# Chains between products: scaling of the stream on VectorE, a root of the mean per token on a 128x2 tile, sums turned by halves, and two weight units split ahead

## The reference, cut to what matters

```python
for l in range(2):                                   # first block
    xm = rms_norm(x, norm_mix_w[l]) * (1 + sc1) + sh1
    proj = xm @ w_in[l]                              # q, k, v, pool, gates: 4096 columns
    ...                                              # attention, pooling, gates
    x = x + g1 * (merged @ w_out[l])
    xf = rms_norm(x, norm_ffn_w[l]) * (1 + sc2) + sh2
    x = x + g2 * peer_ffn(xf, ...)                   # query, top-k, all 16384 experts as dense products
x = rms_norm(x, final_norm_w)

def post_norm_update(x, y, gate, res_w, g, b):       # second block: after each of six sub-layers
    return layer_norm(ALPHA * x + res_w * gate * y, g, b)
# per layer: half-step FFN, mixer (neighbourhood attention in layer 0, short convolution in layer 1), half-step FFN
# FFN: (silu(a) * u) @ w_out with a, u = split((x * (1 + scale) + shift) @ w_in); in layer 0 the context passes the first FFN too
```

## Time and profile before

| | us |
|---|---|
| median of 3 runs | 3928.18 |
| lowest and highest run | 3926.26, 3933.19 |
| profiled execution, its own time | 3927.0 |
| its span, first to last instruction | 3925.1 |
| TensorE busy / VectorE / ScalarE / GpSimd | 3737.5 / 2533.5 / 2049.0 / 231.4 |

### The profile page before, as it was taken

How to read it: one execution, slowest core, us unless ns; L and a number is a source line. 1 busy time by engine, 2 the same in 40 slices (tenths; PEclk the granted TensorE clock), 3 DMA queues, 4 the chain that set the end, 5 groups by cost and what they waited for, 6 DMA issues and landing times.

```text
span 3925.1 us, 75611 instructions
## 1 busy us (share of the span) xinstructions
PE 3737.5 (95%) x26204; PEld 3326.8 (85%) x26204; DVE 2533.5 (65%) x4978; ACT 2049.0 (52%) x4251; POOL 231.4 (6%) x328
## 2 busy tenths in 40 slices
PE   6999999999999999999999999899999989898898
PEld 1889888998888889888988888799988789898897
DVE  0665686556777565586556777576657566666765
ACT  1555446776555555445776555444544444444444
POOL 0000011110000000011110000110001010101100
PEclk9999999999999999999999999899999999999999
DMA  8334788777777434688776777655544045453353
GB/s 307 132 127 162 252 302 276 248 247 237 241 241 236 137 124 160 235 295 287 251 242 238 241 241 241 194 182 167 187 145 145 30 145 185 135 186 134 129 187 129
DMA packets 245135, 782.60 MB, mean 199 GB/s; under 512 B 29888, under 2 KB 63040, under 8 KB 244672
## 3 DMA queue, kind: packets, MB, share of 16 engines
q1 hardware_dynamic: 230976, 738.65, 56.7%
q0 software_dynamic: 13952, 41.14, 2.9%
HBM read 745.07 MB, written 34.60 MB: 199 GB/s over the span
## 4 chain that ended last, share of the span: by engine, by line
PE 77%; PEld 6%; DVE 6%; DMA 4%; issue 3%; ACT 2%; PEldq 1%; SPq 0%; ACTq 0%; DVEq 0%; POOL 0%
PE bank L1705 17%; PE bank L1706 16%; PE bank L1707 16%; PE bank L1760 5%; PE bank L1761 5%; PE bank L1762 5%; DMA raw<-stream 3%; PE bank L1977 3%; PE bank L1845 3%; PEld bank L1762 2%; PEld bank L1760 2%; PEld bank L1761 2%; DVE wl L987 2%; PE bank L1823 2%; PE bank L1961 1%
## 5 line engine op out<-in xcount | busy, mean ns | idle before, releaser
L987 DVE TENSOR_TENSOR wl<-raw,wh 128x512 fp32r<-128x512 f32 x2180 | 1482.9, 702 | 879.7 <-ACT wh L565 876.4
L565 ACT ACTIVATE wh<-raw 128x512 fp32r<-128x512 f32 x2180 | 1317.6, 628 | 956.4 <-PE bank L1762 436.9
L1705 PE MATMUL bank<-XH,wh 128*128 128x256 f32 x5184 | 1517.7, 293 | 104.0 <-DVE XL L1088 49.1
L1706 PE MATMUL bank<-XL,wh 128*128 128x256 f32 x5184 | 1480.2, 286 | 0.0
L1707 PE MATMUL bank<-XH,wl 128*128 128x256 f32 x5184 | 1479.0, 285 | 0.0
L1705 PEld LDWEIGHTS bank<-XH,wh 128*128 128x128 f32 x5184 | 1005.2, 194 | 166.1 <-issue 84.1
L1706 PEld LDWEIGHTS bank<-XL,wh 128*128 128x128 f32 x5184 | 1009.2, 195 | 4.2 <-issue 1.0
L1707 PEld LDWEIGHTS bank<-XH,wl 128*128 128x128 f32 x5184 | 1007.4, 194 | 0.0
L1760 PE MATMUL bank<-wh,AH 128*128 128x512 f32 x1464 | 571.3, 390 | 1.1 <-DVE AL L1437 1.1
L1761 PE MATMUL bank<-wl,AH 128*128 128x512 f32 x1464 | 570.9, 390 | 0.0
L1762 PE MATMUL bank<-wh,AL 128*128 128x512 f32 x1464 | 569.6, 389 | 0.0
(11 more groups left out here) (222 smaller groups left out, 3113.5 us busy)
## 6 DMA issues: line engine op xcount, KB each, us to landing
raw<-stream SPq DMA_DIRECT2D x1340, 512.0 KB, 4.2
h_spill<-side POOLq DMA_DIRECT2D x256, 128.0 KB, 3.9
side<-h_spill SPq DMA_DIRECT2D x256, 128.0 KB, 3.8
arena<-rpb POOLq DMA_DIRECT2D x4, 1024.0 KB, 22.2
arena<-tables POOLq DMA_DIRECT2D x2, 832.0 KB, 7.2
X<-x_t SPq DMA_DIRECT2D x1, 1024.0 KB, 7.5
arena<-ctx_t POOLq DMA_DIRECT2D x1, 1024.0 KB, 8.5
out_t<-X SPq DMA_DIRECT2D x4, 256.0 KB, 2.3
```

What stands on the lines that cost most here:

```text
L565: act.activation(wh[:, n % 4, :], raw[:, q % 4, HALF * half:HALF * (half + 1)], ACT.Copy).then_inc(hi_ready, 1)
L987: tt_op(wl[:, n % 4, :], raw[:, q % 4, HALF * half:HALF * (half + 1)], wh[:, n % 4, :].bitcast(F32), SUB).then_inc(lo_ready, 1)
L1705: pe.matmul(out, wh[:, n % 4, a:b], moving_h, start=start, stop=False, skip_group_check=check)
L1706: pe.matmul(out, wh[:, n % 4, a:b], moving_l, start=False, stop=False, skip_group_check=check)
```

## The change

- **Stream scaling.** The multiply by factor and root moves from GpSimd to DVE (`update_view`, one `scalar_tensor_tensor` of 128x256 for each tile). It is put between weight units of the next stage: in FFN stages behind feature tiles 1 to 4 (11 to 14 in `ffn.0.0`), in `qkv` and `conv_in` between units. GpSimd keeps only the addition of the shift, 48 times 128x256.
- **Root per token.** Before `w_in`, `query`, in the four `layer_norm` and at the end, each square tile is now the stationary operand, in two halves of 128 tokens, and one column of the 1/1024 matrix is moved (`token_square`). The sum lies in a 128x2 tile, tokens on partitions. ACT takes the root of 128x2, DVE inverts 128x2, and TensorE spreads it to 128x256 in the same bank by a product with the unit matrix (`spread_over`). DVE reads the spread root from PSUM. In the second block a second copy is spread to bank 0, and ACT copies it to the arena for `update_view` (`keep_spread`). The other four norms, inside `ffn.0.0`, `ffn.0.0.x`, `kv_ctx` and their hooks, keep the old way.
- **Tables.** `take_table` runs a one-element activation so that the table is loaded there: Sqrt ahead of the squares, and Sigmoid, Gelu or Silu right behind the root.
- **Sums by halves.** Transposes of the first halves start once ACT's and DVE's first copies are there; `sum_turned` is raised after each two tiles, and DVE waits per two tiles.
- **First two units.** Unit 1 of the next stage is split before the chain ends (`hi` behind the copies or inside the product before, `lo` ahead of the reciprocal). The first two units are taken in sequence (`opened`).
- **Small edits.** Coefficients and biases are computed earlier.

```diff
@@ gpsimd
-            pool.tensor_tensor(X[:, :, :], X[:, :, :], spread(A(RMS2, T), KT), ALU.mult).then_inc(view_step, 1)
-            pool.wait_ge(view_step, n + 1)
             for k in range(KT):
-                factor, shift = view_coef[:, 0, k:k + 1], view_coef[:, 1, k:k + 1]
-                pool.tensor_scalar(X[:, k, :], X[:, k, :], factor, shift, ALU.mult, ALU.add).then_inc(view_ready, 1)
+                pool.wait_ge(view_step, KT * n + k + 1)
+                pool.tensor_scalar(X[:, k, :], X[:, k, :], view_coef[:, 1, k:k + 1], None, ALU.add)\
+                    .then_inc(view_ready, 1)
@@ scalar
+        def take_table(func):
+            act.activation(small[:, UNREAD:UNREAD + 1], eps[:, 0:1], func)
+        def token_root(bank, func):
+            act.wait_ge(stat_ready, seen("stat_ready"))
+            act.activation(small[:, TOKEN_RMS:TOKEN_RMS + TT], bank[:, 0:TT], ACT.Sqrt, bias=eps[:, 0:1])\
+               .then_inc(rms_ready, 1)
+            take_table(func)
+        def keep_spread(bank, dst, updates):
+            act.wait_ge(view_ready, 1 + KT * updates)
+            act.wait_ge(kept_spread, seen("kept_spread"))
+            act.activation(dst, bank[:, 0:T], ACT.Copy).then_inc(rms_copied, 1)
...
-        def layer_norm(updates):
+        def layer_norm(updates, func=ACT.Silu):
             seen("stat_ready")
+            take_table(ACT.Sqrt)
             squares(X, ZSQ, centred, "centred")
-            stream_root(banks[7][:, 0:T], updates)
+            token_root(banks[7], func)
+            if updates < 6:
+                keep_spread(banks[0], rms, updates)
...
         copy_sum()
+        hi(stages["ffn.1.0"], 1)
         layer_norm(3)
@@ vector
+        def token_invert():
+            dve.wait_ge(rms_ready, seen("rms_ready"))
+            dve.reciprocal(small[:, TOKEN_INVERSE:TOKEN_INVERSE + TT], small[:, TOKEN_RMS:TOKEN_RMS + TT])\
+               .then_inc(inverse_ready, 1)
+            dve.wait_ge(rms_spread, seen("rms_spread"))
+        def update_view(ks):
+            for k in ks:
+                dve.scalar_tensor_tensor(X[:, k, :], X[:, k, :], view_coef[:, 0, k:k + 1], rms, MUL, MUL)\
+                   .then_inc(view_step, 1)
...
-            dve.wait_ge(sum_turned, seen("sum_turned"))
             for k in range(KT):
-                dve.scalar_tensor_tensor(view[:, k, :], banks[k // 2][:, (k % 2) * T:(k % 2 + 1) * T], factor(k),
-                                         view[:, k, :], MUL, ADD).then_inc(semaphore, 1)
+                if k % 2 == 0:
+                    dve.wait_ge(sum_turned, seen("sum_turned"))
+                dve.scalar_tensor_tensor(view[:, k, :], turned_sum(k), factor(k), view[:, k, :], MUL,
+                                         ADD).then_inc(semaphore, 1)
...
+        def layer_norm(then):
             centre(X_)
-            invert(rms)
-            operand(X_, modul, factor, shift, rms)
+            lo(then, 1)
+            token_invert()
+            operand(X_, modul, factor, shift, banks[7][:, T:2 * T])
+            dve.wait_ge(rms_copied, seen("rms_copied"))
@@ tensor
+        def token_square(sq, bank, kept=None):
+            for k in range(KT):
+                pe.wait_ge(squares_ready, seen("squares_ready"))
+                for tt in range(TT):
+                    last = pe.matmul(bank[:, tt:tt + 1], A(sq + k * T + tt * P, P), mean_d[:, 0:1],
+                                     start=k == 0 and tt == 0, stop=k == KT - 1 and tt == 1, skip_group_check=True)
+            last.then_inc(stat_ready, 1)
+            pe.wait_ge(inverse_ready, seen("inverse_ready"))
+            spread_over(bank, T, rms_spread)
+            if kept is not None:
+                spread_over(kept, 0, kept_spread)
+        def spread_over(bank, first, done):
+            for tt in range(TT):
+                at = TOKEN_INVERSE + tt
+                last = pe.matmul(bank[:, first + tt * P:first + (tt + 1) * P],
+                                 small[:, at:at + 1].broadcast_to([P, P]), ident[:, :], start=True, stop=True)
+            last.then_inc(done, 1)
```

More of the change, by code:

```diff
@@ L375, in build @@
     acc_done = sem("acc_done")
-    sum_copied = sem("sum_copied")
+    sum_copied = [sem(f"sum_copied{i}") for i in range(TT)]
     sum_turned = sem("sum_turned")
@@ L585, in step @@
                 take(k, i, per)
+            if opened:
+                hi(st, 2)
+                take(0, 0, 0)
+                take(1, 0, 0)
+                a = 2
+            count = b - a - (b == st.units)
             rounds = count // 4 if count >= 8 else 0
@@ L603, in to_arena, with pairs @@
             return evacuate
-        def pairs(st, nin, func, hooks=None, then=None):
+        def pairs(st, nin, func, hooks=None, then=None, opened=False):
             count = FF_TILES
@@ L846, in _ @@
                 copy_sum()
+            hi(stages["ffn.0.0" if l else "w_in.1"], 1)
         ctx_tiles, modul, rms = tiles(CTX, KT), tiles(TMP, KT), A(RMS2, T)
@@ L872, in _ @@
             hooks[6 + n] = lambda n=n: operand((2 * n, 2 * n + 1), modul, shift_of(0, 0, 0), second_pair)
-        pairs(stages["ffn.0.0"], 2, ACT.Silu, hooks, then=stages["ffn.0.0.x"])
+        pairs(stages["ffn.0.0"], 2, ACT.Silu, hooks, then=stages["ffn.0.0.x"], opened=True)
         def context_squares():
@@ L1004, in one @@
                 take(k, i, per)
+            if opened:
+                lo(st, 2)
+                take(0, 0, 0)
+                take(1, 0, 0)
+                a = 2
+            count = b - a - (b == st.units)
             rounds = count // 4 if count >= 8 else 0
@@ L1437, in row_lows @@
                 tt_op(AL[:, j % 2, :], AP_[:, j % 2, :], AH[:, j % 2, :].bitcast(F32), SUB).then_inc(row_ready, 1)
+            if l == 0:
+                add_bias(1, 1, 12)
+                scale_plus_one(scale[:, :], mod1[:, 1, 8:16], column("norm_mix.1", 0, KT))
+            else:
+                for n in range(DEPTH):
+                    add_bias(n, 2, 30)
             dve.wait_ge(gate_banks_free, 2 + BATCHES * (l + 1))
@@ L1537, in _ @@
         hooks.update(pieces(6, X_, rms, lambda k: mod2[:, 0, k:k + 1, 0], second_pair))
-        pairs(stages["ffn.0.0"], 2, ffn_combine, hooks, then=stages["ffn.0.0.x"])
-        residual_factor(0, 0, 1, 0.5)
+        for n in range(4):
+            hooks[11 + n] = lambda n=n: update_view((2 * n, 2 * n + 1))
+        hooks[15] = lambda: residual_factor(0, 0, 1, 0.5)
+        pairs(stages["ffn.0.0"], 2, ffn_combine, hooks, then=stages["ffn.0.0.x"], opened=True)
         dve.wait_ge(view_ready, 1)
@@ L1640, in layer_norm, with ffn, coefficients_after @@
             stream_coefficients(*name)
+        def layer_norm(then):
             centre(X_)
[L1642 to L1647 removed]
+            lo(then, 1)
+            token_invert()
+            operand(X_, modul, factor, shift, banks[7][:, T:2 * T])
+            dve.wait_ge(rms_copied, seen("rms_copied"))
+        def ffn(name, l, which, updates, then, after=None):
+            def coefficients_after():
+                residual_factor(l, 0 if which == 0 else 48, 0, 0.5)
+                if after is not None:
+                    dve.wait_ge(view_ready, 1 + KT * updates)
+                    coefficients(l, which, *after)
+            hooks = {n + 1: lambda n=n: update_view((2 * n, 2 * n + 1)) for n in range(4)}
+            hooks[8] = coefficients_after
+            pairs(stages[name], 2, ffn_combine, hooks, then=then, opened=True)
             dve.wait_ge(view_ready, 1 + KT * updates)
             stream_sum(factor_of_sum, X_, evacuated)
+        coefficients(0, 1, 0, 48)
         product(stages["na_o"], residual(lambda k: scale[:, bass.ds(k, 1)]), then=stages["ffn.0.1"])
[L1652 to L1656 removed]
+        layer_norm(stages["ffn.0.1"])
+        ffn("ffn.0.1", 0, 2, 3, stages["ffn.1.0"], (1, 0))
+        layer_norm(stages["ffn.1.0"])
+        ffn("ffn.1.0", 1, 0, 4, stages["conv_in"], (1, 24))
+        layer_norm(stages["conv_in"])
         st = stages["conv_in"]
```

121 lines of the change are left out of this document (68 added, 53 removed).

## The result

| | median us | ratio to before, 95% interval | span of the profiled execution | mean clock |
|---|---|---|---|---|
| before | 3928.7 | | 3925.1 | 0.982 |
| after | 3900.2 | 0.9927, 0.9910 to 0.9944 | 3899.6 | 0.976 |

The kernel is faster by 28.5 us, where the sum had 44.9 (3882); 3900.2 lies 1.2 above the slow end of the range, 3899.

A forecast was written before the change was run, and what follows sets the result against it. TensorE was busy 3737.5 of 3925.1 us, so its idle 187.6, largely waits at chains between products, was what could be won. Stage gains of 45.9 less 1.0 gave 44.9: 3927.0 to 3882 us, range 3864 to 3899.

The forecast's parts named there:

- Halves: Ahead of `ffn.1.0`, `conv_in` and at the end: additions start earlier when the sum is turned by halves, gain 1.53 us.
- Mean square: In the chains: 32 one-column records at 0.114 us take 3.65 instead of 3.72, gain 0.07 us.
- Table: Between mean square and root: the load now done ahead of the squares, gain 1.28 us; none at `query`, `w_in`, `ffn.1.1`.
- Rival C: A pause as long as the load behind each of nine table loads following a root: 11.5 us lost, 3894; chance 6%.
- Root: In the chains: the root takes 0.20 us for two columns instead of 0.47 for 256, gain 0.27.
- Root to first high part: Root's end to `XH`: ScalarE's load decides, 1.96 us with the kept copy (gain 0.39), 1.55 without (gain 0.86; 0.74 at end).
- Multiply and unit 1: At the next stage's first units: GpSimd's multiply gone and unit 1 ready save 3.25 us waiting and 1.0 low clock, 4.25.
- What the multiply becomes: In six stages: VectorE's eight scalings of 0.44 us each are mostly hidden, costing 1.0 us for all stages together.
- rival B: In six stages GpSimd's additions and VectorE's new work obstruct each other, 0.6 us for each of 24 pairs: 3897; chance 12%.
- A: In nine chains one-column matmuls are quick, half of 0.114 us a record: 12.4 us more gained, 3870; chance 18%.
- E: The mean square's 32 records run one after the other at 0.40 us each: 82 us more, 3964, slower; chance 4%.
- D: At the first units the lock stays and VectorE is still held: 25 us of gain missing, 3907; chance 5%.

The follow-up runs named there:

- number 2: Changed kernel with mean square, root and reciprocal back at 256 columns in the stream's layout in all nine chains; 3889.8 us, ratio 0.9899 to the kernel before.
- number 5: Changed kernel with the turn by halves undone: all 16 transposes wait for all four copies, the additions for all transposes; 3908.9 us, ratio 0.9947 to the kernel before.
- number 8: Changed kernel without the table loads ahead of the squares, so the root loads its own table again; 3901.5 us, ratio 0.9921 to the kernel before.
- number 3: Changed kernel with the token mean square's 16 matmuls moving 128 columns of the mean matrix instead of one; 3894.1 us, ratio 0.9910 to the kernel before.

## Why the prediction was wrong

**The step that failed is the price of the form per token: the clock under the mean square and the spread.** The sum priced both in records at 2.4 GHz and asked about the clock only at the first units. It gave the form per token, over the 256-column form with all else equal, some 7.6 us of gain (0.07 + 0.27 in seven chains, 0.39 four times, 0.86 twice, 0.74 at the end, 1.2 at `w_in.1`); number 2 shows 11 to 14 us of loss. That is 19 to 21 us, and the forecast missed by 18. In the stream's chains and at the end the root starts 1.50 to 3.35 behind the squares in the two traces of the changed kernel (1.56 with 256 columns), and root to `XH` takes 2.71 (forecast 1.96; 1.79 at the full clock).

How much of this the clock explains is another matter. These chains gained 24.5 and 25.9 us where 30.8 were forecast, and 31.6 with 128 columns at the full clock: the clock took some 6 to 7 us there, and that is shown. A second part has no term in the sum at all: `expert_u` lost 7.7 and 11.0 us in the two traces, of which up to 4.8 is the unchanged kernel's own scatter, and its cause stays open. Smaller parts are 2.5 us up to `w_out.0`, 1.5 and 2.9 in `w_in.1`, and 3.0 and 3.5 behind the first units of `qkv` and in the attention.

Term by term:
- *Halves*: 1.53 forecast, 1.46 measured (number 5). Right.
- *Mean square*: 3.65 us forecast, a gain of 0.07; 3.73 at the full clock (number 5), so right there, and a loss of 1.4 ahead of `ffn.1.0` in after.
- *Table*: 1.28, right in size, but by another cause (number 8). Rival C is out: the root ends at 3359.69, the load runs from 3359.71 to 3360.99, the next activation starts at 3361.00. The Trainium skill (ScalarE: Activation LUTs, "What ACT_TABLE_LOAD costs") adds a drain of 1.38 us to each load; the trace does not agree, as no such gap stands behind this load or behind 43 others of the 50 in after.
- *Root*: 0.27 forecast, 0.21 measured (0.47 to 0.26).
- *Root to first high part*: at the full clock the way was not ScalarE's load alone: 1.79 with the kept copy and 1.52 without. At the low clock the eight spread records decided. The sum counted the four records of one spread and forgot that the kept copy waits for the other four.
- *Multiply and unit 1*: 4.25 forecast at four places. The wait is gone from the trace (no low part over 0.93 us from 3343 to 3399), but the clock's 1.0 was not won: the low clock of the chain reached over unit 1, the case named with its end of 0.
- *What the multiply becomes*: 1.0 forecast, 2.0 found, in `qkv` alone, where GpSimd's additions took 1.81 us beside VectorE's rotations, and 0.92 to 1.09 in the other five stages. This was rival B in one of its six stages. The lock of the Trainium skill (SBUF — State Buffer, "SBUF: two separate sides") agrees in kind with the 1.81: the two engines hold each other up.
- *`ffn.0.0`*: 4.8 forecast, 5.0 and 5.1 measured. *`ffn.0.0.x` and `kv_ctx`*: 2.9 against 2.7, of it 0.8 in the first and 1.9 in the second. *`qkv`*: 3.6 against 4.3. *`query`*: 1.2 each, 1.0 and 0.2. *`ffn.1.1`*: 5.0 against 2.6 and 3.1.
- *Rivals*: A and E are out by number 5, C by the rows, D by the vanished waits; B holds at one stage, with 2.0 us and not its 14.

The range was too narrow at its slow end because the clock was a term at four places and not a condition on the other terms, and because stages that the change does not enter had no term and no scatter.

## What to carry to other kernels

Price a chain between products at both clock levels: a smaller matmul saves nothing if the clock falls under the steps that follow. Before dropping work from the engine whose clock matters, try the wider form that costs nearly the same: here 128 columns ran in 3.84 us where one column took 3.73 at the full clock and up to 6.3 below it, and they kept the mean square and the spread at 2.4 GHz. And take two traces of the kernel before; here two `expert_u` stages differed by 2.9 and 1.9 us between two executions of the same kernel.

## What the runs showed of the hardware

- A record of a matmul of one column with a new 128x128 load of weights takes 0.117 us at the full clock (number 5), one of 128 columns 0.120 (3.84 for 32, number 3): the 127 further columns cost 0.003 us.
- Eight 128x128 records take 1.16 us at 2.4 GHz (number 3) and 2.08 at 1.2 (after).
- Behind the first record of a mean square with one moved column the granted clock fell to 1.2 GHz after 0.8 to 4.6 us, at all eight chains of seven traces; with 128 or 256 columns after 5.8 us at the earliest, in seven traces.
- A table load starts without waiting for the semaphore of its own activation where that has a single wait (1.28 us beside the mean square in number 8), and behind the waits where there are two. This is how the two always fell together here; nothing else tested it.
- A 128x256 addition on GpSimd took 0.92 to 1.09 us in the FFN stages and `conv_in`, and 1.81 beside VectorE's rotations in `qkv`.
